# Differential attention: values as plain fp32 matmuls on unsplit operands, turned probabilities copied out by VectorE, and each head's query tiles in falling order

## What is computed

```python
def block(i):                       # one tile of Q_BLOCK = 128 queries
    qb = lax.dynamic_slice_in_dim(q, i * Q_BLOCK, Q_BLOCK, axis=1)
    qpos = i * Q_BLOCK + jnp.arange(Q_BLOCK)
    s = jnp.einsum('bqhcd,bkhcd->bhcqk', qb, k).astype(jnp.float32) * scale
    s = jnp.where(kpos[None, :] <= qpos[:, None], s, NEG_INF)
    p = jax.nn.softmax(s, axis=-1)
    a = p[:, :, 0] - lam * p[:, :, 1]
    return jnp.einsum('bhqk,bkhe->bqhe', a.astype(v.dtype), v)
```

## Time and profile before

| | us |
|---|---|
| median of 3 runs | 2003.43 |
| the three runs | 2014.6, 2003.34, 2003.43 |
| span of the profiled execution | 2010.5 |
| attention stage in it, first scores to last values | 1089.5 to 1193.5 |

### The profile page before, as it was taken

How to read it: one execution, slowest core, us unless ns; L and a number is a source line. 1 busy time by engine, 2 the same in 40 slices (tenths; PEclk the granted TensorE clock), 3 DMA queues, 4 the chain that set the end, 5 groups by cost and what they waited for, 6 DMA issues and landing times.

```text
span 2010.5 us, 25493 instructions
## 1 busy us (share of the span) xinstructions
PE 1979.7 (98%) x10112; PEld 1672.2 (83%) x10112; DVE 1045.0 (52%) x1607; ACT 810.0 (40%) x1474; POOL 283.0 (14%) x290
## 2 busy tenths in 40 slices
PE   7999999999999999999999999999999999999998
PEld 7888988888888888888988788788888888888887
DVE  6765665554363222334554866876775543322333
ACT  5542543343353222333324862466664333222332
POOL 1001000000000000000003742377751000000000
PEclk9999999999999999999999998999999999999999
DMA  6331333333323333332543143221126423333321
GB/s 211 105 105 57 113 104 96 101 98 95 95 95 105 95 95 102 97 95 64 158 145 96 48 159 119 79 64 48 48 64 209 117 72 115 95 97 103 95 95 73
DMA packets 60261, 202.22 MB, mean 101 GB/s; under 512 B 8336, under 2 KB 8368, under 8 KB 59760
## 3 DMA queue, kind: packets, MB, share of 16 engines
q1 hardware_dynamic: 56080, 185.10, 29.5%
q0 software_dynamic: 4064, 15.49, 2.3%
HBM read 181.16 MB, written 8.39 MB: 94 GB/s over the span
## 4 chain that ended last, share of the span: by engine, by line
PE 93%; DVE 2%; DMA 1%; ACT 1%; issue 1%; DVEq 1%; POOL 1%; POOLq 0%; ACTq 0%; SPq 0%
PE ps L700 27%; PE ps L702 27%; PE ps L701 27%; PE ps L1203 2%; PE ps L1192 1%; PE ps L1119 1%; PE ps L1241 1%; PE ps L1240 1%; PE ps L1193 1%; PE ps L792 1%; POOL PU L656 1%; DMA w2v<-in_w2v 0%; DVE XN L1884 0%; PE ps L1048 0%; PE ps L1037 0%
## 5 line engine op out<-in xcount | busy, mean ns | idle before, releaser
L1844 DVE TENSOR_TENSOR Wl<-raw,Wh 128x1024 fp32r<-128x1024 f32 x307 | 378.2, 1234 | 690.7 <-ACT Wh L1324 689.3
L700 PE MATMUL ps<-HTh,Wh 128*128 128x512 f32 (+1 forms) x1712 | 644.7, 377 | 3.0 <-DVE gst L2437 1.1
L702 PE MATMUL ps<-HTh,Wl 128*128 128x512 f32 (+1 forms) x1712 | 637.5, 372 | 0.0
L701 PE MATMUL ps<-HTl,Wh 128*128 128x512 f32 (+1 forms) x1712 | 637.3, 372 | 0.0
L1324 ACT CAST Wh<-raw 128x1024 fp32r<-128x1024 f32 x307 | 321.7, 1051 | 740.3 <-DMA raw<-in_w_all 740.1
L700 PEld LDWEIGHTS ps<-HTh,Wh 128*128 128x128 f32 x1712 | 323.7, 189 | 57.5 <-issue 2.1
L702 PEld LDWEIGHTS ps<-HTh,Wl 128*128 128x128 f32 x1712 | 322.9, 189 | 56.5
L701 PEld LDWEIGHTS ps<-HTl,Wh 128*128 128x128 f32 x1712 | 323.3, 189 | 53.1
L700 PE MATMUL ps<-Wh,Yh 128*128 128x512 f32 x528 | 205.8, 390 | 0.0
L702 PE MATMUL ps<-Wh,Yl 128*128 128x512 f32 x528 | 205.5, 389 | 0.0
L701 PE MATMUL ps<-Wl,Yh 128*128 128x512 f32 x528 | 205.4, 389 | 0.0
(11 more groups left out here) (288 smaller groups left out, 2390.1 us busy)
## 6 DMA issues: line engine op xcount, KB each, us to landing
raw<-in_w_all SPq DMA_DIRECT2D x307, 512.0 KB, 3.5
swp_d<-qkd SPq DMA_DIRECT2D x64, 64.0 KB, 2.9
g_dram<-gst SPq DMA_DIRECT2D x16, 256.0 KB, 3.9
ring<-g_dram POOLq DMA_DIRECT2D x16, 256.0 KB, 3.5
X<-in_x SPq DMA_DIRECT2D x4, 512.0 KB, 6.2
swp_r<-qkr SPq DMA_DIRECT2D x16, 128.0 KB, 3.6
gpre<-in_g_pre POOLq DMA_DIRECT2D x4, 512.0 KB, 4.3
Kh<-Kh SPq DMA_DIRECT2D x16, 128.0 KB, 2.4
```

Of the source, the lines that this page charges most:

```text
L700: tensor.matmul(dst, a_hi, b_hi, start=start, stop=False)
L701: tensor.matmul(dst, a_hi, b_lo, start=False, stop=False)
L702: return tensor.matmul(dst, a_lo, b_hi, start=False, stop=stop)
L1844: vector.tensor_tensor(Wl[:, s, :], raw[:, s, :], Wh[:, s, :], ALU.subtract).then_inc(w_lo, 1)
```

## The change

The values are formed by one plain fp32 matmul per key tile, straight from `vd` and from one unsplit copy `ATd` of the turned probabilities. `ATdh`, `ATdl`, `Vst`, `high`, `v_high`, `v_low` and the wait on `v_low` are gone. The copy out of PSUM is DVE's (`turned_out`), in the place where `low` stood. Because values are now read from `vd` itself, on whose bytes the output goes, the tiles of a head run in falling order: widths 512, 384, 256, 128. POOL's `qk_low` waits for the turn of a step where it waited for the `high` of the same step, and `exps(t)` on ACT waits for turn t - 2 itself.

```diff
+        ATd = at("ATd", 72, [P, 2, SEQ])
-        ATdh = at("ATdh", 72, [P, 2, 1, SEQ], F32R)
-        ATdl = at("ATdl", 76, [P, 2, 1, SEQ], F32R)
...
+        def tile_of(t):
+            return 3 - t % 4
+
         def width(t):
-            return (t % 4 + 1) * P
+            return (tile_of(t) + 1) * P
...
                     if head >= 2:
-                        pl.wait_ge(at_hi, 4 * (head - 2) + 3)
+                        pl.wait_ge(full[4], FILLED["da"][4] + 2 * (head - 2) + 2)
...
             def values(t):
-                u, n = t % 2, t % 4 + 1
+                u, n = t % 2, tile_of(t) + 1
                 b = 6
                 bank_free("da", b, t)
-                if t % 4 == 0:
-                    pe.wait_ge(st_lo, v_parts(t // 4))
+                head = t // 4
                 bank_free("da", 4 + u, t // 2 + 1)
                 for j in range(n):
-                    a = slice(j * P, (j + 1) * P)
-                    last = three(ps[b][:, 0:P], ATdh[:, u, 0, a], ATdl[:, u, 0, a], Vst[:, t // 4 % 2, 0, a], Vst[:, t // 4 % 2, 1, a],
-                                 j == 0, j == n - 1)
+                    last = tensor.matmul(ps[b][:, 0:P], ATd[:, u, j * P:(j + 1) * P], vd[:, j, head * P:(head + 1) * P],
+                                         start=j == 0, stop=j == n - 1)
                 last.then_inc(full[b], 1)
...
             def exps(t):
+                if t >= 2:
+                    filled("da", 4 + u, (t - 2) // 2)
...
-            def low(t):
+            def turned_out(t):
 
                 w = width(t)
                 u = t % 2
-                ve.wait_ge(at_hi, t + 1)
-                vector.tensor_tensor(ATdl[:, u, 0, 0:w], ps[4 + u][:, 0:w], ATdh[:, u, 0, 0:w], ALU.subtract).then_inc(free[4 + u], 1)
+                filled("da", 4 + u, t // 2)
+                at_least(ve, full[6], FILLED["da"][6] + t - 1)
+                vector.tensor_copy(ATd[:, u, 0:w], ps[4 + u][:, 0:w]).then_inc(free[4 + u], 1)
```

More of the change, by code:

```diff
@@ L185, in program @@
         kal = at("kal", -8, [P, 2, SEQ], F32R)
-        Vst = at("Vst", -8, [P, 2, 2, SEQ], F32R)
         vhl = [at("vhl0", -8, [P, TT, 2, P], F32R), at("vhl1", 92, [P, TT, 2, P], F32R)]
@@ L333, in program @@
         a_ready = sem("a_ready")
-        at_hi = sem("at_hi")
         qk_hi = sem("qk_hi")
@@ L387, in qk_parts @@
         def qk_parts(head):
-            return (0, 4)[head] if head < 2 else 5 * head - 1
-        def v_parts(head):
-            return min(9 + 5 * head, 40)
+            return 4 * head
         def q_parts(head):
-            return (0, 2)[head] if head < 2 else 3 * head - 1
-        def v_casts(head):
-            return min(5 + 3 * head, 24)
+            return 2 * head
         def nsf_ends(t):
@@ L585, in qk_low @@
                         pool.tensor_tensor(Qst[other, u, m, :], q[own, :], Qst[own, u, m, :], ALU.subtract).then_inc(st_lo, 1)
[L587 to L593, removed]
                 pl.wait_ge(roped, 8 + 16)
@@ L603, in _ @@
                 qk_low(0, 1)
-                v_low(0, 0)
                 for head in range(2, 8):
                     qk_low(0, head)
-                    v_low(0, head - 1)
-                v_low(0, 7)
                 if on("cmp"):
@@ L843, in scores @@
             def scores(t):
-                i, u, b2 = t % 4, t // 4 % 2, 2 * (t % 2)
+                i, u, b2 = tile_of(t), t // 4 % 2, 2 * (t % 2)
                 w = width(t)
                 q = slice(i * P, (i + 1) * P)
-                if i == 0:
+                if t % 4 == 0:
                     pe.wait_ge(st_lo, qk_parts(t // 4) + 4)
@@ L1486, in exps @@
                                       accum_out=rs[:, u, m:m + 1]).then_inc(free[b], 1)
[L1488 to L1494, removed]
             def da_out(t):
                 filled("da", 6, t)
-                scalar.activation(YD[:, t % 4, span(0, 2 * P, t // 4 * P, P)], ps[6][:, 0:P], ACT.Copy,
+                scalar.activation(YD[:, tile_of(t), span(0, 2 * P, t // 4 * P, P)], ps[6][:, 0:P], ACT.Copy,
                                   scale=rr[:, t % STEPS, 0:1]).then_inc(free[6], 1)
@@ L1509, in attention @@
                 exps(0)
-                v_high(0)
                 exps(1)
@@ L1516, in attention @@
                         da_out(t - 2)
-                    high(t)
                     head = t // 4 + 2
@@ L1524, in attention @@
                         q_high(head, 1)
-                    if t % 4 == 0 and t:
-                        v_high(t // 4)
                     if t in HIGH_AT:
@@ L1540, in qk_high @@
                 q_high(head, 1)
[L1542 to L1547, removed]
             ac.wait_ge(boot, 1)
@@ L2065, in attention @@
                     if exists(t - 1):
-                        low(t - 1)
+                        turned_out(t - 1)
                     if exists(t + 2):
@@ L2070, in attention @@
                         split(CHUNK0["vda"] + 7 + LOW_AT.index(t) + LEAD)
-                low(TOTAL - 1)
+                turned_out(TOTAL - 1)
             vector.memset(eps[:], EPS)
```

## The result

The forecast was wrong, in size and in sign. The changed kernel takes 2015.57 us (median of 8 runs, 2012.56 to 2017.12), the kernel before 2003.5 us (8 runs, 2002.2 to 2014.6). The ratio over all runs is 1.0042, 95% interval 1.0024 to 1.006: slower, by less than 1%. (The two medians stand further apart, at 1.0060, because the runs of before lie in two groups and their median in the lower one; the means, 2014.98 and 2006.95, stand at 1.0040.) Forecast were 1997.3 us and a range up to 2004.5.

The account below looks back on a forecast made before the run. TensorE bounds the kernel overall, with DVE nearly the bound in steps 0 to 28 and the bound there afterwards. Terms -3.8 - 3.1 + 0.8 = -6.1 us took the median from 2003.43 to 1997.3 us; range 1991 to 2004.5 (8 in 10).

Parts of the forecast that it names:

- Values on PE: Attention stage: a key tile's product goes from 0.334 to 0.223 us, relieving PE of 8.9 us over 80 tiles.
- The copy at nothing: DVE, attention stage: the PSUM copy replaces the `low` part (mean 0.481 us) at a net cost of 0.
- PE's wait for `v_low`: PE ahead of the values matmuls: this wait, at most 3.2 us, goes.
- Waits of DVE on POOL, "5 us": Steps 0 to 28: 5 us of DVE's 19.6 us of combine subtractions are waits on POOL, kept unchanged.
- DVE's floor of 74.4 us: Steps 0 to 28: DVE's work stays 74.4 us and bounds the stretch; with 2.2 us of waits, 76.6 us.
- The sign it gave for being wrong: The forecast is wrong if the combine subtraction's mean, 0.701 us before, rises above 0.85 us; two other signs were given.
- "Falling order: no gain or loss in sum": Attention stage: falling tile order leaves the work per head the same; only front, end and the splits' places differ.
- Its terms in front and at the end: Falling order adds 0.8 us ahead of the first transposes; the last three steps lose 3.1 us from 16.8.
- "Nothing changes behind the stage": Behind the attention stage: PE's 3 us idling for `w2v` stays and shifts with the stage; counted at nothing.
- The rival "clock": Behind the stage: most changed runs have the 0.57 clock stretch, most before hadn't; 2004 to 2008 us, chance 0.12.
- the rival "DVE slower": Attention stage: `combine` meets POOL subtractions in three of four steps and waits; +7.7, 2011.1 us, chance 0.10.

Follow-up runs that it names:

- early loads: `w2k` and `w2v` loaded before the last `values`, nothing else edited: changed kernel 2004.24 us, kernel before 2003.03 us.
- the corner in which little holds the combine up: Changed kernel with the two loads moved ahead, tiles in rising order, POOL's subtractions left out for heads 2 to 7: 1993.94 us.
- the four corners: Changed kernel, two loads moved ahead, with POOL's subtractions / without in heads 2 to 7: falling order 2004.24 / 1993.70 us, rising order 1994.23 / 1993.94 us.
- the other three corners: Changed kernel, two loads moved ahead: falling order without POOL's subtractions (heads 2 to 7) 1993.70 us; rising order with them 1994.23, without 1993.94.
- runs 9, 10 and 12: Changed kernel, two loads moved ahead, plus: POOL's head work one step later 2003.76 us; copy on ACT 1998.25; copy on ACT and splits one step earlier 1995.46.
- run 11: Changed kernel with the two loads moved ahead, the copy on ACT and POOL's head work one step later: 2009.97 us.
- experiments 1 and 2: Changed kernel, loads not moved: POOL's subtractions left out for heads 2 to 7, 2004.84 us; copy out of PSUM on ACT instead of DVE, 2009.56 us.

## Why the prediction was wrong, point by point

**Values on PE: right.** 160 rows, two pieces for each plain matmul; in the chain eight of them take 0.89 us, 0.11 each. With rising order and early loads, plain matmuls and the copy give 1994.23 - 2003.03 = -8.8 us; 8.9 of PE's time was the relief worked out. That the two are so close is partly luck: PE's 3.1 us of waits behind `v_low` went as well, and its waits for the combine rose from 2.5 to 5.7 us.

**The copy at nothing: right.** 481 ns for the 481 of the low part. What it hid: DVE is where a saving counts, and on ACT the copy would have given 6.0 us.

**PE's wait for `v_low`: right.** It is gone, from PE's groups and from its waits.

**Waits of DVE on POOL, "5 us": the step that failed.** The forecast kept the 5 us of before because "which of them meets a `combine` changes". It had named the new pair, the 512-wide combine with the key low parts, and put no price for it into the sum. With the 551 ns of the corner in which little holds the combine up, the stage had 32 x (713 - 551) ns = 5.2 us of such waits before, as the forecast had it, and has 32 x (895 - 551) ns = 11.0 us after. In steps 0 to 28 the price was 6.8 us of combine and 0.8 of splits, where nothing was forecast: DVE's floor of 74.4 us became about 81, while its idle time fell by 3.7 as forecast (3.8). The sign it gave for being wrong, a mean above 0.85 us, came in at 0.944. The size of a meeting was right as well: the rival priced it at up to 1.0 us, and the rows show 0.6 (1.37 for 0.75) and 1.0 (1.62 for 0.62). The Trainium skill, "SBUF — State Buffer", section "SBUF: two separate sides", has the rule that decides it: an exclusive lock between a DVE operation with two SBUF inputs and a GpSimd one that reads SBUF, held for the whole instruction. The trace agrees: the combine, with both inputs in SBUF, is held for 0.6 to 1.0 us. That is 0.2 us less than a wait for POOL's end and the whole undisturbed time behind it would give (0.83 + 0.75 = 1.58 us for 1.37, 1.20 + 0.62 = 1.82 for 1.62), so a small part of the instruction is not held up. The copy at 1120.89, whose input is in PSUM, takes its 0.28 us while `Qst` runs beside it.

**"Falling order: no gain or loss in sum": wrong, for the same reason.** Its terms in front and at the end were nearly right. The front took 7.55 us for 6.8 (forecast +0.8), the last steps 14.35 for 16.8 (forecast 13.7). The waits of PE for the combine were forecast to be longest behind steps 6, 10, 14 and 22; they are 0.49 us there and up to 0.99 ahead of the wide tiles, where POOL stands. But the order sets who stands beside POOL: +10.0 us by the four corners.

**The sum.** The span was forecast at 2004.4 and is 2010.9, +6.5. Of that +6.7 is steps 0 to 28, +0.6 the last steps, +0.4 a later start of the stage, and -1.2 what lies behind it, of which PE's shorter idling for `w2v` is about 1 us.

**"Nothing changes behind the stage": wrong in the median.** Taking 7.1 us off the profiled execution assumed that the changed kernel runs at full clock as often as before. It never did. From the forecast span of 2004.4 to 1997.3 the offset is -7.1; from the measured span of 2010.9 to 2015.57 it is +4.7. That is 11.8 of the 18.3 us by which the forecast missed, the larger part, and 6.5 is the span, nearly all of it the stage. The rival "clock" had this mechanism, at a chance of 0.12, and the rival "DVE slower" the other, at 0.10. Both came at once, with a DVE part milder than its 2011.1; the forecast had the two together only for a loss of 20 us (0.02).

**What stays open.** Why the changed kernel has the half-clock stretch each time and the one before in 32 of 77 runs. Early loads show that the idling ahead of `cmp_hidden` is what lets it happen: without it, none of 20 runs of the two kernels has it, nor, by their mean clock of 0.998 to 1.0, has any of the 35 runs of the other three corners and of runs 9, 10 and 12; run 11 has its low clock inside the stage. With the idling, all 28 runs of the changed kernel and of experiments 1 and 2 have a mean clock of 0.994 to 0.996; their profiles show 2.1, 4.5 and 3.3 us of it, the one of before 3.0. No profile was taken of a run of before at full clock. The 0.6 to 1.1 us that early loads took off those runs suggest that they idle for less than 3.0 us, and the transfer of `w2v`, which ends the idling, is not steady (9.1 us in the profile of before, 6.0 in the changed kernel). That this is what parts the two groups is not shown.

## What to carry to other kernels

When a change reorders the work of one engine, list which of its operations will run beside which of the other engine of a shared lock, and price each pair: a narrow operation that waits costs little, a wide one in the busiest step is on the path at its full length. A clean test of "order or contention" is four corners; effects that don't add are one effect. And where the runs of a kernel come in two groups, find what parts them before comparing medians: here, moving two loads kept both kernels at full clock in every run, and only that made the 1.2 us of the change visible.

## What the runs showed of the hardware that was not expected

The hold works both ways. DVE's split of 1024 columns (both inputs in SBUF) made POOL's cast of 64 x 512 take 1.33 us for 0.60, in the two neighbouring rows at 1115.29 and 1116.13; the split itself took 1.42 for 1.22. So it also delays POOL's chain and moves which combine is hit next: in the four heads with such a split the 128-wide combine takes 0.35 us, in the two without it meets POOL and takes 0.75 and 0.76.

A wait of 2 us on PE in the middle of a stage costs more than 2 us. In run 11, matmuls of the scores waited up to 2.0 us for `Qst`, six times for 8.7 us in all, and the granted clock of the stretches around them was 0.83 to 0.87; ahead of `cmp_hidden`, 2.1 us of idling were followed by 14.7 us at 0.56, which cost 12.46 - 7.25 = 5.2 us in one group of matmuls alone. The Trainium skill, "TensorE: Matmul & The Clock Gate", section "What's actually happening", has the gate granting one of two clocks, 1.2 or 2.4 GHz, by how busy PE has been; by it a value between 0.5 and 1 in a stretch is a mean of both. The rows agree; busy time by stretch of the changed kernel, the clock third from the end:

```profile
1220.00:1225.00 5.00, 5.00 (x25) 5.00 (x25) 3.37 (x4) 1.53 (x2) 4.57 (x6) 0.50 0.45 132
1225.00:1230.00 5.00, 5.00 (x24) 4.90 (x24) 3.21 (x5) 0.40 (x2) 1.35 (x2) 0.50 0.17 41
1230.00:1235.00 5.00, 5.00 (x19) 3.97 (x18) 4.83 (x6) 1.66 (x1) 0.00 (x0) 0.76 0.00 2
1235.00:1240.00 5.00, 5.00 (x41) 4.77 (x39) 0.66 (x1) 1.83 (x4) 0.00 (x0) 1.00 0.47 129
```

The clock is at half for ten microseconds, and the 0.76 is the stretch in which it rises again.

A narrow fp32r matmul is a poor bargain; this the forecast had read from the trace, and the runs bear it out. At 128 columns it costs 0.111 us and a plain fp32 one 0.223, so that three of the first cost half as much again as one of the second.
